# Moving the attention logits one row further ahead on TensorE, and signalling the normed rows by halves

## The chip, the core and the metric

The kernel runs on one core of a Trainium2 chip. The metric is device time in microseconds (us) for one execution. Five engines work side by side, each through its own list of instructions in order: TensorE (PE in the profile: matrix products and transposes; PEld is its loading of weights), VectorE (DVE), ScalarE (ACT), GpSimd (POOL) and SyncE (SP, which issues DMA transfers). They meet only at semaphores: one instruction counts a semaphore up when it is done, another waits for a count.

## What is computed

One layer of a streaming encoder over 1024 rows of 1024 features, all in float32. Cut to the part around the change:

```python
h = rms_norm(x, mix_norm_g)
u_a, v_a, q, k, v = split(h @ w_in)
y_a = spatial_gating(u_a, v_a, ...)
# sliding-window attention, 8 heads, chunks of 64 rows, windows of 128 keys
logits = einsum(q, k) * 64 ** -0.5 + bias
p = softmax with a learned sink per head (logits)
y_b = einsum(p, v)
x = x + concat(rms_norm(y_a), rms_norm(y_b)) @ w_out
h = rms_norm(x, ffn_norm_g)
x = x + (silu(h @ w_gate) * (h @ w_up)) @ w_down
return rms_norm(x, final_norm_g)
```

## The kernel before, in words

The program is written by hand, engine by engine: each engine's function is a straight list of calls, and their order in the source is the order on the engine. The 1024 rows are 8 row tiles of 128 (T = 8). A product of two float32 matrices is made of three matmuls of rounded parts (`split_mm`, lines 853 to 855).

After the input projection comes a loop over the row tiles r = 0 to 7, the output stage, in which the attention of coming rows, the output projection of rows r and r+1 and the transposes of the normed row r-1 are interleaved. On TensorE one turn of it, for r from 1 to 5, is:

- `probs_T(r+1, 0)`, `out_unit(r+1, 0)`, `probs_T(r+1, 1)`: the probabilities of row r+1 transposed in two parts (line 1033), with 12 matmuls of the output projection between them (`out_unit`: the first half of the features, `ya`, against `woA`, units 0 and 1; the second, `yb`, against `woB`, units 2 and 3).
- `yb_rows(r)`: one transpose (line 1051) for the norm of the attention's output.
- `logits(r+2)`: 8 small products of queries and keys (line 1021), into two PSUM banks.
- `h2_transposed(r-1, 0)`: four transposes of the first 512 columns of the normed row `x2n` (line 1116).
- `out_unit(r+1, 1)`, `values(r+1)` (probabilities times values, line 1044), `h2_transposed(r-1, 1)` (the other 512 columns), `out_unit(r, 2)`, `out_unit(r, 3)`.

The turn r = 0 has only `out_unit(1, 1)`, `values(1)`, `out_unit(0, 2)`, `out_unit(0, 3)`; its logits stand ahead of the loop. The turn r = 6 has no logits.

On VectorE the same turn is `norm_x2(r-1)` (line 2036: row r-1 times its root and gain, 1024 columns into `x2n`), `add_out(r+1, 0)` (line 2024: a projected half added into the row `xr`), `yb_totals(r)` (line 2006), `add_bias(r+2)` (line 1973: the logits read out of PSUM into the tile `S`) and `maxima(r+2)` (lines 1984 to 1988), `h2_lo(r-1, 0)` (line 2043, or 2049 from row 4 on: what is left of the transposed row after rounding), `add_out(r+1, 1)`, `yb_lo(r+1)` (line 2002), `add_out(r, 2)`, `normal_probs(r+2)` (lines 1993 to 1998, which end with `S` ready to be transposed), `h2_lo(r-1, 1)`, `add_out(r, 3)`. In the turn r = 0, `woB_piece` (line 2010) and `ya_lo_rows` (line 1883) stand among them.

A row's way from projection to transposes is a chain over four engines: `out_unit(r, 3)` on PE, `add_out(r, 3)` on DVE, `x2_square(r)` on ACT (line 1502), the root on POOL (lines 647 and 649), `norm_x2(r)` on DVE, `h2_transposed(r, 0)` on PE.

The waits that count here:

- `h2_transposed(r, kh)` waits for `x2n_ready` at r+1 (the last row, r = 7, has a signal `x2n_half` of its own for kh = 0), and for the PSUM bank: `h2_ready` at 2r + kh, which `h2_lo` of the part before counts up, since all these transposes go through bank 7.
- `logits(r)` waits for `s_added` at 2r + 1, that is, until `add_bias(r-1)` has read the two banks.
- `probs_T(r, 0)` waits for `pn_ready` at r+1, from `normal_probs(r)`.

Of the kernel before, what the change touches and what calls it, by code (L numbers as in the profile page):

```python
# [24 lines left out]
def hybrid_trunk_layer(nc, x, xT, mix_gT, w_in, sgu_ln_g, sgu_ln_b, sgu_w, sgu_b, sinks, rel_bias,  # L25
                       group_norm_g, w_out, ffn_norm_g, w_gate, w_up, w_down, final_norm_g, out):
    F32, F32R = mybir.dt.float32, mybir.dt.float32r
    ALU, ACT, AX = mybir.AluOpType, mybir.ActivationFunctionType, mybir.AxisListType
    P = 128
    ROWS, D = x.shape  # L30
    T = ROWS // P
# [16 lines left out]
    C = 512  # L48
# [5 lines left out]
    def at(name, kb, shape, dtype=F32):  # L54
        n = 4
        for s in shape[1:]:
            n *= s
        offset = BASE + int(kb * 1024)
        assert offset + n <= nc.sbuf_usable_end, name
        return nc.alloc_sbuf_tensor_at(name, shape, dtype, offset=offset)  # L60
# [60 lines left out]
    xr = [at(f"xr{s}", a, [P, D]) for s, a in enumerate((160, 164, 26))]  # L121
    x2n = at("x2n", 196.25, [P, D])
    ffn_gB = at("ffn_gB", 202, [P, D])
# [64 lines left out]
    ssq2, ms2, rstd2 = late[:, 0:T], late[:, T:2 * T], late[:, 2 * T:3 * T]  # L188
# [51 lines left out]
    def added_at(p, i):  # L240
        return 4 * ADDED.index(p) + i + 1

    def corner_at(p, i):
        return 4 + 4 * CORNERS.index(p) + CORNER_ORDER[p].index(i) + 1
# [17 lines left out]
    def out_at(r, n):  # L262
        return OUT.index((r, n)) + 1
# [37 lines left out]
    with ExitStack() as ctx:  # L301
        ps = ctx.enter_context(nc.psum_tensor("ps", [P, 8, C], F32))

        def sem(name):
            return ctx.enter_context(nc.semaphore(name))
# [36 lines left out]
        out_done, out_added, x2_sq, ms2_ready, rstd2_ready, x2n_ready, h2_T, h2_ready = (  # L342
            sem(n) for n in ("out_done", "out_added", "x2_sq", "ms2_ready", "rstd2_ready", "x2n_ready", "h2_T",
                             "h2_ready"))
# [12 lines left out]
        x2n_half = sem("x2n_half")  # L357
# [491 lines left out]
        def _(pe):  # L849
# [157 lines left out]
            def logits(r):  # L1007
                if r == 0:
                    pe.wait_ge(c_out, corner_at("P3", 1))
                    pe.wait_ge(vwin_ready, 4)  # L1010
                else:
                    pe.wait_ge(s_added, 2 * r + 1)
                if r == HT:
                    pe.wait_ge(c_out, corner_at("P4", 1))
                for ci in range(2):
                    c = 2 * r + ci
                    for tp in range(2):
                        for g in range(KV):
                            rows = slice(g * DH, (g + 1) * DH)
                            q = qT[r // HT][rows, c % (NCH // 2), 2 * tp:2 * tp + 2, :].rearrange("p t q -> p (t q)")  # L1020
                            last = mm(ps[:, 3 + g, (2 * ci + tp) * P:(2 * ci + tp + 1) * P], q, kT[rows, c * CH:c * CH + WIN],  # L1021
                                      start=True, stop=True)
                last.then_inc(logits_done, 1)

            def probs_T(r, ci):
                pe.wait_ge(pn_ready, r + 1)
                if r == 0 and ci == 0:
                    pe.wait_ge(c_summed, added_at("P3", 2))
                if ci == 1:
                    pe.wait_ge(pT_ready, 2 * r + 1)  # L1030
                for g in range(KV):
                    for tp in range(2):
                        last = nc.tensor.transpose(ps[:, 5, (2 * g + tp) * P:(2 * g + tp + 1) * P], S[:, g, ci, tp, :], ident[:])  # L1033
                last.then_inc(p_T, 1)

            def values(r):
                pe.wait_ge(pT_ready, 2 * r + 2)
                if r:
                    pe.wait_ge(yb_totalled, r)
                else:  # L1040
                    pe.wait_ge(c_summed, added_at("P3", 3))
                for ci in range(2):
                    for g in range(KV):
                        last = mm(ps[g * DH:(g + 1) * DH, 6, ci * G * CH:(ci + 1) * G * CH], V2[:, 2 * r + ci, g, :], pT[:, ci, g * G * CH:(g + 1) * G * CH],  # L1044
                                  start=True, stop=True)
                last.then_inc(pv_done, 1)
# [29 lines left out]
            def out_unit(r, n):  # L1076
                u = out_at(r, n) - 1
                h = n % 2
                if u >= 3:
                    pe.wait_ge(out_added, u - 2)  # L1080
                else:
                    pe.wait_ge(c_out, corner_at("P4", u))
                if n < 2:
                    if u == 0:
                        pe.wait_ge(wo_split, HA)
                    if r % HT == 0:
                        pe.wait_ge(ya_ready, 8 if r else 4)
                    lhs = [ya[:, r, hl] for hl in range(2)]
                    rhs = (woA_hi, woA_lo)
                else:  # L1090
                    pe.wait_ge(yb_ready, r + 1)
                    lhs = [yb[r % 2][:, hl] for hl in range(2)]
                    rhs = (woB_hi, woB_lo)
                cs = slice(h * C, (h + 1) * C)
                for k in range(4):
                    if n == 2 and r == 0:
                        pe.wait_ge(wo_split, HA + k + 1)
                    last = split_mm(ps[:, u % 3, :], (lhs[0][:, k, :], lhs[1][:, k, :]), (rhs[0][:, k, cs], rhs[1][:, k, cs]), k == 0, k == 3)
                last.then_inc(out_done, 1)

            def h2_transposed(r, kh):
                if r == T - 1 and kh == 0:
                    pe.wait_ge(x2n_half, 1)
                else:
                    pe.wait_ge(x2n_ready, r + 1)
                if r == T - 2 and kh:
                    pe.wait_ge(out_added, out_at(T - 2, 3))
                elif r == T - 1:
                    pe.wait_ge(out_added, out_at(T - 1, 2 + kh))
                elif r or kh:  # L1110
                    pe.wait_ge(h2_ready, 2 * r + kh)
                else:
                    pe.wait_ge(ssqA_ready, 2)
                for k in range(4):
                    a = (4 * kh + k) * P
                    last = nc.tensor.transpose(ps[:, H2_BANK[r, kh], k * P:(k + 1) * P], x2n[:, a:a + P], ident[:])  # L1116
                last.then_inc(h2_T, 1)
# [9 lines left out]
            for r in range(T):  # L1127
                if 0 < r < T - 1:
                    probs_T(r + 1, 0)
                    out_unit(r + 1, 0)  # L1130
                    probs_T(r + 1, 1)
                    yb_rows(r)
                if 0 < r < T - 2:
                    logits(r + 2)
                if r + 1 < T:
                    if 0 < r < T - 2:
                        h2_transposed(r - 1, 0)
                    out_unit(r + 1, 1)
                    if r == T - 2:
                        h2_transposed(r - 1, 0)  # L1140
                    values(r + 1)
                    if 0 < r < T - 2:
                        h2_transposed(r - 1, 1)
                out_unit(r, 2)
                if r == T - 2:
                    h2_transposed(r - 1, 1)
                if r == T - 2:
                    yb_rows(r + 1)
                out_unit(r, 3)
# [597 lines left out]
        def _(dve):  # L1747
            tt, ts, stt = nc.vector.tensor_tensor, nc.vector.tensor_scalar, nc.vector.scalar_tensor_tensor
# [277 lines left out]
            def norm_x2(r):  # L2026
                if r == 0:
                    dve.wait_ge(ffng_in, 16)
                else:
                    dve.wait_ge(h2_T, 2 * r)  # L2030
                dve.wait_ge(rstd2_ready, r + 1)
                if r == T - 1:
                    stt(x2n[:, 0:C], xr[r % 3][:, 0:C], rstd2[:, r:r + 1], ffn_gB[:, 0:C], ALU.mult, ALU.mult).then_inc(x2n_half, 1)
                    stt(x2n[:, C:D], xr[r % 3][:, C:D], rstd2[:, r:r + 1], ffn_gB[:, C:D], ALU.mult, ALU.mult).then_inc(x2n_ready, 1)
                    return
                stt(x2n[:], xr[r % 3][:], rstd2[:, r:r + 1], ffn_gB[:], ALU.mult, ALU.mult).then_inc(x2n_ready, 1)

            def h2_lo(r, kh):
                flat = "p k n -> p (k n)"
# [74 lines left out]
            for r in range(T):  # L2114
                if r:
                    norm_x2(r - 1)
# [32 lines left out]
            weight_lo(0, "P2", 0)  # L2149
            weight_lo(0, "P6", 0)  # L2150
            norm_x2(T - 1)
            h2_lo(T - 2, 0)
            h2_lo(T - 2, 1)
# [158 lines left out]
```

## Time and profile before

| | before |
|---|---|
| median of 3 runs | 927.34 us (927.29 to 927.34) |
| the profiled execution: time | 927.43 us |
| the profiled execution: span on the core | 925.6 us |
| PE busy | 913.2 us, 99% of the span |
| PEld, DVE, ACT, POOL busy | 81%, 64%, 47%, 43% |
| granted TensorE clock | 0.998 of full speed |
| output stage, the turns r = 1 to 5 | 190.1 to 267.0 us of the span |

The profile lists for every engine the instructions with start and length, what ended an idle time before them, and the granted clock. The trace has two records for a float32 matmul that is no product of rounded parts, so 8 products of the source are 16 there. Its matmuls overlap: a start is when one enters the array, and the next may enter before it has left, so what counts for PE is the distance from start to start.

### The profile page before, as it was taken

Reading aid. Unit: us, or ns where it says so; the run is one execution under the profiler, and the core shown is the slowest. Engines: PE = TensorE matmul, PEld = TensorE weight load, DVE = VectorE, ACT = ScalarE, POOL = GpSimd, SP = SyncE. Lnnn points to the kernel's source line nnn. Section 1 sums busy time; section 2 is a strip of 40 time slices with the busy share of each in tenths; the row PEclk is TensorE's granted clock in tenths of the full one; section 3 lists DMA queues with packets and bytes.
Section 4 is the critical chain, followed back from the end, with each engine's and each line's share of the span. In section 5 each row is a group of like instructions: output and inputs, shape, how many; then the busy total and the mean of one; then the engine's idle time right before and its main releaser. Section 6 shows DMA issues by size and latency. Waiting matters only on the chain.

```text
span 925.6 us, 11960 instructions
## 1 busy us (share of the span) xinstructions
PE 913.2 (99%) x4229; PEld 748.9 (81%) x4229; DVE 588.2 (64%) x776; ACT 430.5 (47%) x837; POOL 402.2 (43%) x392
## 2 busy tenths in 40 slices
PE   9999999899999999999999999999999999999997
PEld 7888887677878878888888888888888888888885
DVE  5659878877677876364464745646446666544753
ACT  6647547775655633332333333333334354444351
POOL 2459633622224388566585564955754000000022
PEclk9999999999999999999999999999999999999999
DMA  9787454112233352725527355273457996656543
GB/s 332 252 242 229 115 162 145 35 57 80 89 108 101 114 170 92 243 88 194 174 98 240 99 174 183 91 239 121 152 190 265 350 385 197 199 189 199 187 139 133
DMA packets 151487, 158.56 MB, mean 171 GB/s; under 512 B 27576, under 2 KB 109060, under 8 KB 151428
## 3 DMA queue, kind: packets, MB, share of 16 engines
q1 hardware_dynamic: 150756, 157.40, 52.5%
q8 instruction: 34, 0.56, 0.2%
q10 hardware_dynamic: 672, 0.40, 0.1%
q14 instruction: 25, 0.20, 0.1%
HBM read 117.26 MB, written 40.50 MB: 170 GB/s over the span
## 4 chain that ended last, share of the span: by engine, by line
PE 87%; DVE 4%; issue 3%; ACT 3%; POOL 2%; DMA 1%; DVEq 0%; POOLq 0%; ACTq 0%
PE ps L853 27%; PE ps L855 27%; PE ps L854 27%; ACT S L1451 1%; PE ps L969 1%; PE ps L1044 1%; PE ps L1116 1%; PE ps L1021 1%; PE ps L1033 1%; DVE P_lo L2086 1%; DMA A22s<-in_w_gate 1%; DVE woA_lo L1780 0%; POOL V L714 0%; PE ps L877 0%; DVE T_lo L2073 0%
## 5 line engine op out<-in xcount | busy, mean ns | idle before, releaser
L2086 DVE TENSOR_TENSOR P_lo<-P_raw,P_hi 128x512 fp32r<-128x512 f32 x132 | 120.8, 931 | 83.5 <-ACT P_hi L1545 76.2
L853 PE MATMUL ps<-T_hi,P_hi 128*128 128x512 f32 x352 | 137.1, 390 | 0.0
L855 PE MATMUL ps<-T_hi,P_lo 128*128 128x512 f32 x352 | 137.0, 389 | 0.0
L854 PE MATMUL ps<-T_lo,P_hi 128*128 128x512 f32 x352 | 136.9, 389 | 0.0
L797 POOL TENSOR_TENSOR wd<-wd 128x256 f32<-128x256 f32 x88 | 81.2, 923 | 93.8 <-DMA wd<-in_w_down 88.6
L853 PE MATMUL ps<-rb_hi,ra_hi 128*128 128x512 f32 x308 | 119.8, 389 | 0.0
L854 PE MATMUL ps<-rb_lo,ra_hi 128*128 128x512 f32 x308 | 119.8, 389 | 0.0
L855 PE MATMUL ps<-rb_hi,ra_lo 128*128 128x512 f32 x308 | 119.8, 389 | 0.0
L1659 ACT ACTIVATE ra_hi<-ra 128x512 fp32r<-128x512 f32 x77 | 48.6, 632 | 98.4 <-DMA rb<-w_down_T 59.6
L647 POOL TENSOR_SCALAR late<-late 128x1 f32<-128x1 f32 x12 | 5.5, 458 | 193.4 <-ACT junk L1727 177.2
L2182 DVE TENSOR_TENSOR ra_lo<-ra,ra_hi 128x512 fp32r<-128x512 f32 x77 | 55.2, 718 | 37.2 <-ACT ra_hi L1659 37.0
L1545 ACT ACTIVATE P_hi<-P_raw 128x512 fp32r<-128x512 f32 x132 | 76.6, 620 | 3.5 <-POOL P_raw L756 3.5
L853 PEld LDWEIGHTS ps<-T_hi,P_hi 128*128 128x128 f32 x352 | 66.1, 188 | 14.3 <-issue 0.7
L855 PEld LDWEIGHTS ps<-T_hi,P_lo 128*128 128x128 f32 x352 | 66.1, 188 | 13.9
L854 PEld LDWEIGHTS ps<-T_lo,P_hi 128*128 128x128 f32 x352 | 66.1, 188 | 13.6
L1650 ACT ACTIVATE G<-G 128x512 f32<-128x512 f32 x33 | 20.9, 632 | 112.4 <-DVE G L2162 112.4
L853 PE MATMUL ps<-B,P_hi 128*128 128x512 f32 x176 | 69.0, 392 | 0.1
L855 PE MATMUL ps<-B,P_lo 128*128 128x512 f32 x176 | 68.5, 389 | 0.0
L854 PE MATMUL ps<-B,P_hi 128*128 128x512 f32 x176 | 68.5, 389 | 0.0
L854 PEld LDWEIGHTS ps<-rb_lo,ra_hi 128*128 128x128 f32 x308 | 57.8, 188 | 12.1
L853 PEld LDWEIGHTS ps<-rb_hi,ra_hi 128*128 128x128 f32 x308 | 57.8, 188 | 12.1
L855 PEld LDWEIGHTS ps<-rb_hi,ra_lo 128*128 128x128 f32 x308 | 57.8, 188 | 11.8
(272 smaller groups left out, 2028.0 us busy)
## 6 DMA issues: line engine op xcount, KB each, us to landing
wd<-in_w_down SPq DMA_DIRECT2D x44, 256.0 KB, 3.4
w_down_T<-wd SPq DMA_DIRECT2D x22, 512.0 KB, 4.8
ra<-act_S SPq DMA_DIRECT2D x44, 256.0 KB, 2.7
rb<-w_down_T SPq DMA_DIRECT2D x44, 256.0 KB, 3.0
act_S<-Q SPq DMA_DIRECT2D x33, 256.0 KB, 3.7
ra<-act_A SPq DMA_DIRECT2D x33, 256.0 KB, 4.9
rb<-in_w_down SPq DMA_DIRECT2D x33, 256.0 KB, 5.7
P_raw<-in_w_gate SPq DMA_DIRECT2D x22, 256.0 KB, 3.6
```

What stands on the lines that cost most here:

```text
L797: nc.gpsimd.tensor_tensor(wd[:, d, :], wd[:, x, :], wd[:, y, :], ALU.subtract).then_inc(wd_summed, 1)
L853: mm(dst, lhs[0], rhs[0], start=start, stop=False, skip_group_check=onto)
L854: mm(dst, lhs[0], rhs[1], start=False, stop=False, skip_group_check=onto)
L855: return mm(dst, lhs[1], rhs[0], start=False, stop=stop, skip_group_check=onto)
L969: last = mm(ps[:, MIX_BANK[m % 2], t * P:(t + 1) * P], vn[:, h, HT * half + t], sgu_wT[:, h, :], start=True, stop=True)
L1021: last = mm(ps[:, 3 + g, (2 * ci + tp) * P:(2 * ci + tp + 1) * P], q, kT[rows, c * CH:c * CH + WIN], start=True, stop=True)
L1033: last = nc.tensor.transpose(ps[:, 5, (2 * g + tp) * P:(2 * g + tp + 1) * P], S[:, g, ci, tp, :], ident[:])
L1545: actv(w_h[p, m][:], src[:], ACT.Copy).then_inc(w_hi_ready, 1)
L1650: actv(g[:], g[:], ACT.Silu).then_inc(silu_done, 1)
L1659: actv(ra_hi[n][:], ra[n][:], ACT.Copy).then_inc(step_hi, 1)
L2086: tt(w_l[p, m][:], src[:], w_h[p, m][:].bitcast(F32), ALU.subtract).then_inc(w_split, 1)
L2182: tt(ra_lo[n][:], ra[n][:], ra_hi[n][:].bitcast(F32), ALU.subtract)
```

## The change

Two things are edited. On TensorE the call of `logits` moves: in the turn r it was `logits(r+2)` behind `yb_rows(r)`; now it is `logits(r+3)` behind `values(r+1)`, also in the turn r = 0, and not in the turn r = 5. On VectorE `norm_x2` writes its row in two halves of 512 columns for every row, the first of which counts up `x2n_half`, the second `x2n_ready`; `h2_transposed(r, 0)` waits for the first. The places of the transposes in the list stay as they are.

```diff
             def h2_transposed(r, kh):
-                if r == T - 1 and kh == 0:
-                    pe.wait_ge(x2n_half, 1)
+                if kh == 0:
+                    pe.wait_ge(x2n_half, r + 1)
                 else:
                     pe.wait_ge(x2n_ready, r + 1)
...
                     yb_rows(r)
-                if 0 < r < T - 2:
-                    logits(r + 2)
                 if r + 1 < T:
...
                     values(r + 1)
+                    if r + 3 < T:
+                        logits(r + 3)
                     if 0 < r < T - 2:
                         h2_transposed(r - 1, 1)
...
                 dve.wait_ge(rstd2_ready, r + 1)
-                if r == T - 1:
-                    stt(x2n[:, 0:C], xr[r % 3][:, 0:C], rstd2[:, r:r + 1], ffn_gB[:, 0:C], ALU.mult, ALU.mult).then_inc(x2n_half, 1)
-                    stt(x2n[:, C:D], xr[r % 3][:, C:D], rstd2[:, r:r + 1], ffn_gB[:, C:D], ALU.mult, ALU.mult).then_inc(x2n_ready, 1)
-                    return
-                stt(x2n[:], xr[r % 3][:], rstd2[:, r:r + 1], ffn_gB[:], ALU.mult, ALU.mult).then_inc(x2n_ready, 1)
+                stt(x2n[:, 0:C], xr[r % 3][:, 0:C], rstd2[:, r:r + 1], ffn_gB[:, 0:C], ALU.mult, ALU.mult).then_inc(x2n_half, 1)
+                stt(x2n[:, C:D], xr[r % 3][:, C:D], rstd2[:, r:r + 1], ffn_gB[:, C:D], ALU.mult, ALU.mult).then_inc(x2n_ready, 1)
```

On PE in the turn r = 0 the list around `values(1)` gains the logits of row 3 (a line number, the result and the operands stand in each row; `qT_152` holds the queries of rows 0 to 3, `qT_153` those of rows 4 to 7):

```order
 L855 MATMUL ps<-woA_hi,ya 128x512
 L1044 MATMUL ps<-pT,V_154 64x256 x4
+L1021 MATMUL ps<-kT,qT_152 128x128 x8
 L853 MATMUL ps<-woB_hi,yb_158 128x512
 L854 MATMUL ps<-woB_lo,yb_158 128x512
```

The eight products stand now between the values and the first matmul of `out_unit(0, 2)`.

On PE in the turn r = 1, and in the same way in r = 2 to 4, the row of logits goes from between `yb_rows` and the first transposes of `x2n`:

```order
 L1033 MATMUL ps<-ident,S 128x128 x4
 L1051 MATMUL ps<-ident,yb_sum_162 128x128
-L1021 MATMUL ps<-kT,qT_152 128x128 x8
 L1116 MATMUL ps<-ident,x2n 128x128 x4
 L853 MATMUL ps<-woA_hi,ya 128x512
```

The transposes of `x2n` follow directly on the single transpose of `yb_rows`. In the turn r = 5 the same row goes too, and none comes back behind its values.

On DVE, the row `x2n` of r = 0 (in the turn r = 1; the others alike):

```order
 L1883 TENSOR_TENSOR ya<-vn,ya 128x4x128 x4
-L2036 SCALAR_TENSOR_TENSOR x2n<-xr_172,late,ffn_gB 128x1024
+L2032 SCALAR_TENSOR_TENSOR x2n<-xr_172,late,ffn_gB 128x512
+L2033 SCALAR_TENSOR_TENSOR x2n<-xr_172,late,ffn_gB 128x512
 L2024 SCALAR_TENSOR_TENSOR xr_174<-ps,small,xr_174 128x512
 L2006 TENSOR_REDUCE small<-ps 128x1
```

One instruction of 1024 columns is now two of 512; ACT, POOL and SP keep their lists.

## Rows read from the trace of the kernel before

**Rows 1.** The page: busy time of each engine.

```profile
PE 913.2 (99%) x4229; PEld 748.9 (81%) x4229; DVE 588.2 (64%) x776; ACT 430.5 (47%) x837; POOL 402.2 (43%) x392
```

**Rows 2.** Waits between 170 and 290 us: us in total, times, longest.

```profile
PE ps L1051 <- POOL yb_sum L774: 2.0, 1, 2.0
...
PEld ps L1033 <- DVE S L1998: 0.9, 2, 0.5
...
PEld ps L853 <- DVE woB_lo L2010: 0.4, 1, 0.4
PE ps L1116 <- DVE x2n L2036: 0.2, 1, 0.2
```

**Rows 3.** The stretch of turn 3: length, busy PE, PEld, DVE, ACT, POOL, clock.

```profile
220.99:236.26 15.27, 15.27 (x91) 12.10 (x89) 10.37 (x18) 9.21 (x28) 3.48 (x7) 1.00 0.19 70
```

**Rows 4.** Timeline of PE, turn 3: start, us, line, operation.

```profile
224.63 0.27 PE L1051 MATMUL ps<-ident,yb_sum 128*128 128x128 f32 x1
224.83 1.16 PE L1021 MATMUL ps<-kT,qT 64*128 64x128 f32 x16
225.92 0.66 PE L1116 MATMUL ps<-ident,x2n 128*128 128x128 f32 x4
...
229.27 1.08 PE L1044 MATMUL ps<-pT,V 128*64 128x256 f32 x8
230.29 0.66 PE L1116 MATMUL ps<-ident,x2n 128*128 128x128 f32 x4
```

**Rows 5.** Timeline of DVE, turn 3.

```profile
224.27 1.29 DVE L2036 SCALAR_TENSOR_TENSOR x2n<-xr,late,ffn_gB 128x1024 f32<-128x1024 f32 x1 [2.22 <-POOL late L649]
225.47 0.75 DVE L2024 SCALAR_TENSOR_TENSOR xr<-ps,small,xr 128x512 f32<-128x512 f32 x1
...
226.33 1.28 DVE L1973 TENSOR_TENSOR S<-ps,bias 128x512 f32<-128x512 f32 x2
...
229.18 0.68 DVE L2043 TENSOR_TENSOR B<-ps,B 128x512 fp32r<-128x512 f32 x1
```

**Rows 6.** Timeline of POOL, turn 3, behind the root of line 649.

```profile
226.50 0.19 POOL L647 TENSOR_SCALAR small<-small 128x1 f32<-128x1 f32 x1 [2.34 <-DVE small L2006]
```

**Rows 7.** Timeline of PE, turns 0 and 1.

```profile
185.83 0.40 PE L854 MATMUL ps<-woB_lo,yb 128*128 128x512 f32 x1
186.07 0.39 PE L855 MATMUL ps<-woB_hi,yb 128*128 128x512 f32 x1
186.44 0.50 PE L853 MATMUL ps<-woB_hi,yb 128*128 128x512 f32 x1
...
189.75 0.39 PE L855 MATMUL ps<-woB_hi,yb 128*128 128x512 f32 x1
190.10 0.66 PE L1033 MATMUL ps<-ident,S 128*128 128x128 f32 x4
...
193.99 1.16 PE L1021 MATMUL ps<-kT,qT 64*128 64x128 f32 x16
195.39 0.65 PE L1116 MATMUL ps<-ident,x2n 128*128 128x128 f32 x4 [0.24 <-DVE x2n L2036]
```

**Rows 8.** Timeline of DVE: turn 0, turn 1 and the last row.

```profile
181.06 1.28 DVE L1973 TENSOR_TENSOR S<-ps,bias 128x512 f32<-128x512 f32 x2
...
194.04 1.28 DVE L2036 SCALAR_TENSOR_TENSOR x2n<-xr,late,ffn_gB 128x1024 f32<-128x1024 f32 x1 [0.52 <-POOL late L649]
...
291.55 1.78 DVE L2033 SCALAR_TENSOR_TENSOR x2n<-xr,late,ffn_gB 128x512 f32<-128x512 f32 x1
293.26 0.74 DVE L2034 SCALAR_TENSOR_TENSOR x2n<-xr,late,ffn_gB 128x512 f32<-128x512 f32 x1
293.92 0.68 DVE L2049 TENSOR_TENSOR T_raw<-ps,T_raw 128x512 f32<-128x512 f32 x1
```

**Rows 9.** Timeline of turn 5: the second transposes on PE, and DVE.

```profile
260.82 0.66 PE L1116 MATMUL ps<-ident,x2n 128*128 128x128 f32 x4
...
259.72 0.68 DVE L2049 TENSOR_TENSOR T_raw<-ps,T_raw 128x512 f32<-128x512 f32 x1
```

## The prediction

> **What bounds the kernel now.** I began with the page: PE is busy 913.2 us of a span of 925.6 [rows 1]. A change can only gain where PE stands still, and can only lose by making it stand. So I then asked for PE's waits in the output stage, where the edits lie [rows 2]. Between 170 and 290 us there are three of note: 2.0 us for `yb_sum` ahead of the loop, which the change doesn't touch, a few tenths for `S` and `woB_lo`, and 0.2 us for `x2n`, once. The windows by turn say the same: turn 3 lasts 15.27 us and PE is busy in all of it [rows 3]. What the change may win is thus well under 1 us; the question is what it may lose. For that I laid the timelines of PE and DVE beside each other.
>
> In turn 3 the single transpose of `yb_rows` starts at 224.63, the logits at 224.83, the first transposes of `x2n` at 225.92 [rows 4]. `x2n` itself is written from 224.27 for 1.29 us, to 225.56 [rows 5]; the writing waited 2.22 us for POOL's root, which hangs on the row's last projection on PE. So the row is ready only 0.36 us before PE asks for it, and it is the 1.09 us of logits (225.92 less 224.83) that cover it.
>
> **Taking the cover away.** The change moves these 1.09 us behind `values`, past the first transposes. No matmul is added or dropped, and a product costs the same at either place unless the neighbours matter (a rival below). But the chain from the last projection of row r-1 to `x2n` is as long as it was, while PE now reaches the transposes 1.09 us earlier against it: at 224.83 in the times of this trace.
>
> **What the halves give back.** The first half is one instruction of 512 columns. Its like in the last row took 0.74 us [rows 8], and `add_out`, of the same kind and size, 0.75 [rows 5]. The other end is the last row's first half, 1.78 us, which ran beside work of POOL [rows 8]; in turn 3 POOL has nothing to do for 2.34 us behind the root [rows 6], so I take 0.75. From the end of such a write to the start of PE there were 0.07 us in turn 1 (194.04 and 1.28 make 195.32, PE at 195.39 [rows 7, 8]). So the transposes start at 224.27 + 0.75 + 0.07 = 225.09, and PE waits 225.09 - 224.83 = 0.26 us where it waited for nothing. Turns 2 to 5 have the same pattern: 4 times 0.26 is 1.04 us. Bounds: 0 if PE is held up by something else until then, 4 times 1.3 if every first half took 1.78.
>
> Turn 1 has less time in hand, since the root came late: PE would arrive at 193.99, and the half is there at 194.04 + 0.75 + 0.07 = 194.86, a wait of 0.87. What goes is the old wait, 195.39 less 195.08 (193.99 and 1.09), 0.31. Net 0.56 us.
>
> **The second half and what is behind it on DVE.** The pair costs more than one write. In the last row the second half started 0.07 before the first had ended, and the next instruction 0.66 after the second's start [rows 8]; a pair of 0.75 thus holds DVE for 0.68 + 0.66 = 1.34, where the whole row held it from 224.27 to 225.47, 1.20 [rows 5]. That is 0.14 us a row for all that is queued behind: `add_out`, `add_bias`, `maxima`, `h2_lo`. The Trainium skill (VectorE: DVE Perf Modes, The DRAIN you can't avoid) says that the next operation doesn't start until the pipe of the one before is empty. By that the pair would hold DVE 0.07 us longer than I reckon, and the one term below in which the pair counts would be 0.69 instead of 0.62; the overlap in the last row speaks against it. Nobody but `h2_lo` is met by PE soon after. It ends at 229.86 in turn 3 [rows 5], 230.07 with the pair and the signal; PE comes to the second transposes at 230.29 less 0.83 (the transposes start that much earlier) plus 1.09 for the logits now in front of them, 230.55. Hidden, by 0.5.
>
> Turn 5 is different: the logits of row 7 were done in turn 4, so none stand in front of the second transposes. PE comes at 260.82 - 0.83 = 259.99; the `h2_lo` it must await ends at 259.72 + 0.68 = 260.40 [rows 9], with 0.14 and 0.07 at 260.61. A wait of 0.62 us. The ends: 0, if DVE gets there sooner, and 0.9, if the transposes lose their 0.26 too.
>
> **What the move wins.** In turn 0, `out_unit(0, 2)` now comes 1.09 us later, when the last piece of `woB_lo` is done. The wait for it was 0.14 us by PE's own starts (0.37 between 186.07 and 186.44, against 0.24 before it [rows 7]) and 0.4 on the weight loads [rows 2]; I take 0.2. Before the next `probs_T` there are 0.35 us from 189.75 to 190.10 [rows 7], 0.12 more than the usual distance, a wait for `S`. It goes as well, since DVE catches up. Together 0.32.
>
> **Waits that the moved logits add.** They need `add_bias(r+2)` done: in turn 3 at 226.33 + 1.28 = 227.61, and PE comes behind `values` at 229.5; in turn 0 at 182.34 [rows 8], and PE at 184.1. Nothing. DMA issues and ACT's and POOL's lists stay; SP's waits for logits are met earlier and stand behind waits for whole rows.
>
> **The sum:** 1.04 + 0.56 + 0.62 - 0.32 = +1.90 us. Nothing later takes it up: behind the loop PE works without waits, and all that it needs hangs on the same rows. The profiled execution took 927.43 us, span 925.6 and 1.8 around it; that makes 929.33. The median of the runs lies 0.09 lower, so I forecast **929.2 us**, 0.2% slower. About 0.2% (1.85 us) is also what a measurement of this kernel can tell from no change: my forecast stands on that edge.
>
> **Rivals.**
> *The halves close the gap.* If PE reaches the first transposes a quarter of a microsecond later than I reckon, or the half is quicker, turns 2 to 5 wait for nothing; then turn 5's second wait is 0.62 + 0.26, and the sum 0.56 + 0.88 - 0.32 = 1.12, 928.4 us: not slower by what can be told. For it speaks that 0.26 is small; against, that the half's 0.75 is measured and that the transpose of `yb_rows` takes only 0.20 [rows 4]. The Trainium skill (Perfetto Trace Analysis, Optimizing Scalar/DVE Operations) backs it: if Vector causes bubbles on other engines, breaking up its instructions may allow work to be completed sooner. By that rule the splitting decides; the rows say that it shortens PE's way by 0.53 us while the move takes 1.09 of cover.
> *The softmax starts sooner*, as logits a row ahead would suggest, and PE's waits for `S` (0.9 us on the weight loads, two of them [rows 2]) vanish with nothing lost: 926.8. Against it: `add_bias` doesn't wait for logits now; DVE runs from `x2n` to it without idle time [rows 5].
> *Neighbours cost.* `values` and logits use the array in other shapes than the transposes. From `values` to the transposes there are 1.02 us, and from the single transpose of `yb_rows` to the logits 0.20 [rows 4]. If the step from `values` to logits pays such a 0.20 once more, the four turns with moved logits lose 0.8, 930.0; at twice that 930.8. It decides wherever the start-to-start is above 1.02.
> *POOL slows the first half* as in the last row: five turns of 1.03, 934. POOL's idle time speaks against it.
>
> **How the numbers follow.** My forecast has 0.62, with its own range 928.6 to 929.8, a little under half of it beyond the edge of 929.2. The closed gap has 0.15, the early softmax 0.03, the neighbours 0.15, POOL or another delay 0.05. Slower: 0.28 + 0.15 + 0.05 = 0.48. Faster by over 0.2% would need 925.5, more than all waits of rows 2 that the change can reach: 0.02. The same: the rest, 0.50. The range 928.0 to 930.6 takes in the closed gap and most of the neighbours.
>
> **What would show it.** In the changed profile: waits of PE's line 1116 for the first half of `x2n` in turns 1 to 5, about 0.9 and four times 0.26; one of some 0.6 for `h2_lo` in turn 5; turns 2 to 4 at 15.5 us instead of 15.27; no wait for `woB_lo`. It is wrong if turns stay at 15.27, if the logits behind `values` take clearly more than 1.09, or if DVE's `add_bias` starts earlier after the row's last projection.

## The result and the profile after

| | before | with the change |
|---|---|---|
| median | 927.65 us (926.87 to 928.58, 21 runs) | 928.95 us (928.14 to 930.49, 21 runs) |
| ratio of the times | | 1.0016, 95% interval 1.0009 to 1.0022 |
| profiled execution: span | 925.6 us | 927.1 us |
| PE busy | 913.2 us, 99% | 912.8 us, 98% |
| granted TensorE clock | 0.998 | 0.996 |

The kernel became slower by 0.8 to 2.0 us. The sum gave 1.90; the forecast of 929.2 lies 0.25 above the median, on a median of before that was 0.3 higher than the three runs shown earlier. Against the 0.2% that the prediction named as the bound of what can be told, the median ratio is just inside "the same"; with 21 runs of each kernel the interval is finer than that bound, and shows a small loss.

The page after has the same instructions on PE, and seven more on DVE for the seven rows now written in two parts:

```profile
span 927.1 us, 11967 instructions
...
PE 912.8 (98%) x4229; PEld 749.5 (81%) x4229; DVE 584.1 (63%) x783; ACT 430.5 (46%) x837; POOL 398.3 (43%) x392
```

The view of waits, PE's rows between 160 and 292 us (us in total, times, longest one), answers to [rows 2]:

```profile
PE ps L1051 <- POOL yb_sum L774: 2.0, 1, 2.0
PE ps L1116 <- DVE x2n L2032: 1.5, 5, 0.8
PE ps L1033 <- ACT pT L1463: 1.1, 1, 1.1
...
PE ps L1116 <- DVE T_raw L2046: 0.7, 1, 0.7
```

Line 1116, the transposes of `x2n`, waited once before, for 0.2 us. Now it waits for the first half (line 2032) five times and once for `h2_lo` (line 2046).

The timelines of turn 3, PE first and then DVE, answer to [rows 4, 5] (start, us, instruction, idle time before it):

```profile
226.36 0.27 PE L1051 MATMUL ps<-ident,yb_sum 128*128 128x128 f32 x1
226.82 0.66 PE L1116 MATMUL ps<-ident,x2n 128*128 128x128 f32 x4 [0.18 <-DVE x2n L2032]
230.15 1.08 PE L1044 MATMUL ps<-pT,V 128*64 128x256 f32 x8
231.16 1.16 PE L1021 MATMUL ps<-kT,qT 64*128 64x128 f32 x16
232.26 0.66 PE L1116 MATMUL ps<-ident,x2n 128*128 128x128 f32 x4
```

```profile
226.01 0.75 DVE L2032 SCALAR_TENSOR_TENSOR x2n<-xr,late,ffn_gB 128x512 f32<-128x512 f32 x1 [2.22 <-POOL late L649]
226.68 0.75 DVE L2033 SCALAR_TENSOR_TENSOR x2n<-xr,late,ffn_gB 128x512 f32<-128x512 f32 x1
227.34 0.74 DVE L2024 SCALAR_TENSOR_TENSOR xr<-ps,small,xr 128x512 f32<-128x512 f32 x1
```

The first half takes 0.75 us and PE starts at 226.82, 0.06 behind its end; the pair holds DVE for 1.33 (226.01 to 227.34), where 1.34 was reckoned. DVE waits 2.22 us for POOL's root as before. The step from `values` to the logits is 1.01 us, from the logits to the transposes 1.10: the neighbours cost nothing. Turns 2 to 4 last 15.54, 15.51 and 15.52 us by the starts of their first transposes; before it was 15.27.

One thing in this profile is not of the change. Behind the 2.0 us wait for `yb_sum`, ahead of turn 0, the matmuls come 0.42 us apart for a while. The windows of that stretch, after the change and then before it (length, busy PE, PEld, DVE, ACT, POOL, granted clock, DMA):

```profile
178.90:182.30 3.40, 3.40 (x12) 2.62 (x10) 3.22 (x5) 0.00 (x0) 1.97 (x4) 0.53 0.02 5
```

```profile
180.20:183.00 2.80, 2.80 (x14) 2.12 (x12) 2.62 (x5) 0.00 (x0) 1.52 (x4) 1.00 0.02 6
```

The same code runs at a granted clock of 0.53, nearly all of it at the lower level of 1.2 GHz, in one profile and at 1.00 in the other. From `yb_rows(0)` to `values(1)` it is 5.04 us after and 3.43 before, 1.61 more. The spans of these two profiles can therefore not be compared as they stand. Their difference of 1.5 us is made of four parts: the profile after reaches the end of the wait 1.28 us earlier (178.37 against 179.65), in code that the edits do not touch; it loses the 1.61; it loses 1.47 from `values(1)` to line 1055 at the end of the output stage; and it is 0.3 shorter behind that. Two experiments below hold the clock still.

### The profile page after: what moved, and what is told of

Read it like the earlier page. It is cut to its first block, busy times and chain, and to the rows that moved or that the text cites. A ratio compares the mean times of both kernels' runs of the same rounds, so it can differ in the third digit from the quotient of the medians.

```text
span 927.1 us, 11967 instructions
## 1 busy us (share of the span) xinstructions
PE 912.8 (98%) x4229; PEld 749.5 (81%) x4229; DVE 584.1 (63%) x783; ACT 430.5 (46%) x837; POOL 398.3 (43%) x392
## 4 chain that ended last, share of the span: by engine, by line
PE 86%; DVE 4%; issue 4%; ACT 3%; POOL 2%; DMA 1%; DVEq 0%; POOLq 0%; ACTq 0%
PE ps L853 27%; PE ps L855 27%; PE ps L854 27%; PE ps L1021 1%; PE ps L969 1%; PE ps L1044 1%; ACT x2n L1502 1%; PE ps L1116 1%; ACT S L1451 1%; DVE P_lo L2083 1%; DVE x2n L2032 1%; DMA A22s<-in_w_gate 1%; DVE woA_lo L1780 0%; PE ps L1033 0%; POOL late L649 0%
## 5 line engine op out<-in xcount | busy, mean ns | idle before, releaser
L2083 DVE TENSOR_TENSOR P_lo<-P_raw,P_hi 128x512 fp32r<-128x512 f32 x132 | 117.1, 903 | 84.8 <-ACT P_hi L1545 77.9
```

What stands on the lines that cost most here:

```text
L2083: tt(w_l[p, m][:], src[:], w_h[p, m][:].bitcast(F32), ALU.subtract).then_inc(w_split, 1)
```

## The experiments

Besides the time, one distance is used: from the start of `values(1)` in turn 0 to the transposes of `yb_raw` (line 1055) in turn 6, all on PE. It was 95.38 us before and 96.85 after.

**The halves alone.** The logits stay where they were; `norm_x2` and the wait are those of the change.

```diff
-                if r == T - 1 and kh == 0:
-                    pe.wait_ge(x2n_half, 1)
+                if kh == 0:
+                    pe.wait_ge(x2n_half, r + 1)
...
-                stt(x2n[:], xr[r % 3][:], rstd2[:, r:r + 1], ffn_gB[:], ALU.mult, ALU.mult).then_inc(x2n_ready, 1)
+                stt(x2n[:, 0:C], xr[r % 3][:, 0:C], rstd2[:, r:r + 1], ffn_gB[:, 0:C], ALU.mult, ALU.mult).then_inc(x2n_half, 1)
+                stt(x2n[:, C:D], xr[r % 3][:, C:D], rstd2[:, r:r + 1], ffn_gB[:, C:D], ALU.mult, ALU.mult).then_inc(x2n_ready, 1)
```

> Only the halves, the logits stay behind yb_rows. Measure beside the time: the stage from the start of values(1) to the transposes of yb_raw (line 1055), 95.38 us before (183.08 to 278.46) and 96.85 with the whole change (183.41 to 280.26). Theory (the move takes away the cover of the chain to x2n, the halves give part of it back): with the cover in place the halves have next to nothing to win. The wait of turn 1 (0.31) goes, but the second transposes of that turn then wait for h2_lo, which the pair puts 0.14 later; stage 95.4, within 0.2 of before, time within 0.03% of before. Rival (the pair's 0.14 on DVE is what costs, in every turn): stage 96.0 or more. Rival (the halves win by themselves): stage 95.1 or less.

Measured: 927.31 us, ratio to before 0.9998 (0.9989 to 1.0007); distance 95.51. No wait for `x2n` is left, and the view of waits has in its place

```profile
PE ps L1033 <- DVE S L1998: 0.5, 2, 0.3
PE ps L1116 <- DVE B L2040: 0.3, 1, 0.3
```

The first row is in turns 0 and 6; the second is the wait of turn 1's second transposes, as expected: by the starts, the halves win 0.32 us ahead of the first transposes of turn 1, and the later `h2_lo` costs 0.31 ahead of the second. With the cover in place the halves win nothing in all.

**The move alone.** The logits as in the change, `x2n` written whole for rows 0 to 6.

```diff
-                if 0 < r < T - 2:
-                    logits(r + 2)
...
                     values(r + 1)
+                    if r + 3 < T:
+                        logits(r + 3)
```

> Only the move of the logits, x2n written whole for rows 0 to 6. Theory: PE now waits for the whole row: turns 2 to 5 lose 0.80 each (x2n ends 1.29 after its start instead of 0.75), turn 1 1.09, no wait for h2_lo in turn 5, and 0.6 won in turns 0 and 6; together +3.7, stage 99.1, time 0.4% above before. Rival (the move costs by its neighbours on the array, whatever x2n does): stage as with the whole change, 96.9. Rival (the move is harmless, the pair costs): stage 95 or less.

Measured: 933.9 us, ratio 1.007 (1.0057 to 1.0083); distance 101.13. The move by itself costs 6.3 us by the medians, and 5.75 by the distance, which leaves out the slow stretch that this profile has too; 3.7 were expected. The waits:

```profile
PE ps L1116 <- DVE x2n L2036: 4.4, 5, 1.3
...
PE ps L1033 <- DVE S L1998: 1.2, 4, 0.3
```

The first row is the expected one: 0.77 to 0.79 us in turns 2 to 5, 1.30 in turn 1. The second was not expected, and the timelines of turn 2 show where it comes from, DVE first and then POOL:

```profile
222.56 0.75 DVE L2024 SCALAR_TENSOR_TENSOR xr<-ps,small,xr 128x512 f32<-128x512 f32 x1 [1.91 <-PE ps L855]
223.22 0.66 DVE L1993 TENSOR_TENSOR small<-small 128x8 f32<-128x8 f32 x1
...
224.15 1.32 DVE L1998 TENSOR_TENSOR S<-S,small 128x1024 f32<-128x1024 f32 x1
```

```profile
223.12 0.74 POOL L770 TENSOR_TENSOR yb_sq<-yb_sq 128x256 f32<-128x256 f32 x1 [7.78 <-ACT yb_sq L1482]
```

An operation on 8 columns, which took 0.16 to 0.17 us in all eight rows before, takes 0.66, until POOL's sum (223.12 to 223.86) is over. That pushes `S` back by 0.5, and `probs_T` waits for `S`: by the starts on PE it costs 0.5 us in each of four turns, which is the 2 us by which the expectation fell short. Before, DVE was already in the multiplication of `S` when POOL's sum came, and POOL was the one held up (1.54 us in turn 2).

**Turn 5's second transposes later.** The change, with

```diff
-                    if 0 < r < T - 2:
+                    if 0 < r < T - 3:
                         h2_transposed(r - 1, 1)
                 out_unit(r, 2)
-                if r == T - 2:
+                if T - 3 <= r < T - 1:
                     h2_transposed(r - 1, 1)
```

> The whole change, with one call more moved: in turn 5 the second transposes of x2n come behind out_unit(5, 2) instead of ahead of it. Theory: the 0.65 us wait for h2_lo in turn 5 goes and nothing takes its place: stage 96.2 (96.85 less 0.65), about 0.8 above before. Rival (the wait only moves on, to what hangs on the later transposes): stage stays near 96.8.

Measured: 928.25 us, ratio 1.0011 (1.0002 to 1.002); distance 96.73. The wait for `h2_lo` is gone and turn 5 takes 14.53 us instead of 15.10. The distance fell by only 0.12, because turn 0 is 0.52 longer in this profile (8.20 us from `values(1)` to `probs_T(2, 0)`, 7.68 with the change): this profile has no slow stretch, and PE waits 0.33 us for `S` there. Against the filled kernel with the change below, whose turn 0 is as long (8.19), the distance is 0.55 shorter (97.28 and 96.73): the wait went and did not move on.

**The first transposes later, in all turns.** As the last, and

```diff
-                    if 0 < r < T - 2:
-                        h2_transposed(r - 1, 0)
                     out_unit(r + 1, 1)
-                    if r == T - 2:
+                    if r:
                         h2_transposed(r - 1, 0)
```

> As e3, and in turns 1 to 5 the first transposes come behind out_unit(r+1, 1), 2.9 us of matmuls later. Theory: all waits for x2n go (turn 1's 0.76, the 0.18 to 0.25 of turns 2 to 5), what the move wins in turns 0 and 6 stays: stage 94.4, time about 0.9 us below before and 2.4 below the change. Rival (the wait goes over to the second transposes, since ACT's copies and h2_lo start later; 0.1 to 0.3 a turn): stage 95 to 95.6.

Measured: 926.39 us, ratio 0.9986 (0.9978 to 0.9995); distance 95.09. No wait for `x2n` is left: with 2.9 us of matmuls in front of the transposes the chain is covered again, and the 1.5 us of these waits in the profile after are gone. The distance is 0.7 above the expected one, by waits for `S` in turns 0 and 6 and one of 0.41 for `h2_lo` in turn 1. It is the first version faster than both kernels; the slow stretch is not in this profile. Part of the gain by the medians is the clock: 10 of these 11 runs have a mean granted clock of 0.998 or more, and only 11 of the 27 of the kernel before. Among such runs alone the medians are 926.37 and 927.00, a gain of 0.6.

**The 2.0 us wait filled, before and after.** In the kernel before, and in the changed one, the wait for `yb_sum` gets matmuls:

```diff
             probs_T(1, 1)
+            pe.wait_ge(ssqA_ready, 1)
+            for n in range(8):
+                mm(ps[:, 7, :], ya[:, 0, 0, n % 4, :], woA_hi[:, n % 4, 0:C], start=True, stop=True)
             yb_rows(0)
```

> The kernel before, with 8 matmuls of 512 columns added on PE ahead of yb_rows(0), whose results nobody reads; they stand in the 2.0 us in which PE waits there for POOL's yb_sum, and take 1.8. It tests a theory on the clock: in three of six profiles so far (the change, e1, e2) the matmuls after this wait come 0.43 us apart instead of 0.23 for some 3.5 us, which costs 1.6; in three (before, e3, e4) they don't. Theory: it is the wait that brings the clock down, by chance of when it falls; with the wait filled no profile has the slow stretch, the median falls by about half of 1.6 (0.5 to 0.8 us below before), and the times of the executions scatter less. Rival (the slow stretch has another cause): the same median as before or later by up to 0.3, the same scatter, a slow stretch in some profiles.

> The whole change with the same 8 matmuls. Theory: again no slow stretch, so that the difference between this and the filled kernel before is the change alone: 1.9 us by the prediction's sum, 1.3 to 2.0 by the marks of the profiles so far; start of turn 1 to line 1055 in the profile 89.2 against 88.4. Rival (the change's loss was mostly the slow stretch): the two filled kernels differ by less than 0.7.

Measured: 926.4 us for the kernel before (11 runs, 926.06 to 927.46; ratio to before 0.9991, 0.9982 to 1.0) and 928.1 for the changed one (11 runs, 927.6 to 928.57; ratio to before 1.0007, 0.9998 to 1.0016). Neither profile has the slow stretch. The windows of it, before and then changed:

```profile
176.60:182.30 5.70, 5.53 (x29) 4.31 (x28) 3.96 (x6) 1.12 (x2) 3.76 (x6) 1.00 0.02 3
```

```profile
176.60:182.30 5.70, 5.53 (x28) 4.10 (x26) 3.96 (x6) 0.93 (x2) 3.73 (x7) 1.00 0.01 3
```

The times scatter over 1.4 and 1.0 us in 11 runs each. Without filling it is 1.5 in the 21 runs of the kernel before that belong to these, and 2.4 in the 21 of the changed one, so that the scatter alone says little for the kernel before. Eight matmuls more made the kernel before 0.9 us faster by the medians (926.4 against 927.29 in the same runs), though the interval just touches no change. Among runs with a mean granted clock of 0.998 or more alone it is 0.5 (all 11 with the filling, 12 of the 21 without), so the clock is part of it; the rest was not followed. Between the filled kernels the medians differ by 1.7 us and the distances by 97.28 - 95.38 = 1.90. With the clock the same, that is the change alone. Behind line 1055 the changed kernel is 0.4 us shorter (646.8 us to the end of the span, 647.2 in the kernel before).

**Turn 0 in another order.** On top of the version with the late transposes: `out_unit(1, 1)` ahead of `yb_rows(0)` on PE, `add_bias(2)` and `maxima(2)` ahead of `yb_totals(0)` on DVE, and the second transposes late in turn 1 too.

```diff
             probs_T(1, 1)
+            out_unit(1, 1)
             yb_rows(0)
...
-                    out_unit(r + 1, 1)
                     if r:
+                        out_unit(r + 1, 1)
                         h2_transposed(r - 1, 0)
...
-                    if 0 < r < T - 3:
+                    if 1 < r < T - 3:
                         h2_transposed(r - 1, 1)
                 out_unit(r, 2)
-                if T - 3 <= r < T - 1:
+                if r in (1, T - 3, T - 2):
                     h2_transposed(r - 1, 1)
...
+                if r == 0:
+                    add_bias(2)
+                    maxima(2)
                 if r + 1 < T:
                     yb_totals(r)
...
-                if r + 2 < T:
+                if 0 < r < T - 2:
                     add_bias(r + 2)
                     maxima(r + 2)
```

> e4, with the 2.0 us wait used: on PE out_unit(1, 1) comes ahead of yb_rows(0) and the transposes of ya_totals; on DVE add_bias(2) and maxima(2) come ahead of yb_totals(0) in turn 0; in turn 1 too the second transposes come behind out_unit(1, 2). Theory: PE's wait for yb_sum goes and the softmax of row 2 no longer hangs behind it: 1.5 to 2.0 us in turn 0, 0.4 in turn 1, and no slow stretch: 2 to 3 us below e4, about 924 us. Rival (DVE's backlog in turn 0 is the bound: the wait moves to values(1) or to probs_T(2, 0)): within 0.6 of e4.

Measured: 923.74 us, ratio 0.9962 (0.9949 to 0.9974), 2.65 below the version with the late transposes, as expected. The wait for `yb_sum` is gone, one of 0.7 for `yb_totals` stands in `values(1)`:

```profile
PE ps L1044 <- DVE small L2005: 0.7, 1, 0.7
```

**The first logits earlier too.**

```diff
-            probs_T(0, 1)
             logits(1)
+            probs_T(0, 1)
```

> e7, and ahead of the loop logits(1) come in front of probs_T(0, 1), where PE waits 1.1 us for ACT's copy of the first probabilities. Theory: the 1.09 us of logits fill that wait: 1.0 below e7. Rival (what hangs on probs_T(0, 1), the copy and values(0), comes as late as it did and PE waits there instead): the same as e7.

Measured: 923.01 us, ratio 0.9953 (0.994 to 0.9965), 0.7 below the last by the medians, with intervals that overlap. PE's 1.1 us wait in `probs_T(0, 1)` became one of 0.7 in `values(0)`:

```profile
PE ps L1044 <- ACT pT L1462: 0.7, 1, 0.7
```

So part of it moved on, as the rival had it. This is the fastest version.

## Why the prediction was right

The mechanism, a cover taken away and half given back, held in turns 1 to 5. Two other steps failed, what turn 0 wins and that nothing later takes the loss up, and the total came out in part by luck: the stage's 1.90 us is what the filled kernels show to the last digit, but with terms that were off and cancel. By the starts on PE in the two filled profiles, from `values(1)` on:

| up to | before | change | added since the row above | predicted |
|---|---|---|---|---|
| `probs_T(2, 0)`, end of turn 0 | 7.00 | 8.19 | 1.19 | 1.09 - 0.32 = 0.77 |
| first transposes of turn 1 | 12.29 | 12.80 | -0.68 | 0.87 - 0.31 - 1.09 = -0.53 |
| first transposes of turn 5 | 73.36 | 74.87 | 1.00 | 4 x 0.26 = 1.04 |
| second transposes of turn 5 | 77.73 | 79.94 | 0.70 | 0.62 |
| `probs_T(7, 0)` | 83.94 | 85.88 | -0.27 | 0 |
| line 1055 | 95.38 | 97.28 | -0.04 | 0 |

- **The cover.** Right: the move alone makes PE wait 0.77 us and more for the whole row, the halves bring that to 0.18 as the view of waits counts it, and 0.25 a turn of start-to-start.
- **What the halves give back.** Right: 0.75 us for the half and 0.06 for the signal, 0.75 and 0.07 predicted. The halves alone changed nothing (0.9998): they are worth something only where the cover is gone.
- **The pair on DVE and turn 5.** Right in place, 0.08 too small: the wait for `h2_lo`, 0.63 in the filled changed kernel, costs 0.70 start to start.
- **What the move wins in turn 0.** This step failed. Its term was -0.32, and the filled kernels show +0.10 (1.19 less 1.09). The wait for `woB_lo` did go, but "DVE catches up" did not hold: in the filled changed kernel PE waits 0.34 us for `S` ahead of `probs_T(2, 0)`.

```profile
PE ps L1033 <- DVE S L2001: 0.3, 1, 0.3
```

  In the filled kernel before, DVE's short operation and then POOL's sum stood like this:

```profile
187.80 0.17 DVE L1996 TENSOR_TENSOR small<-small 128x8 f32<-128x8 f32 x1
```

```profile
188.29 1.77 POOL L770 TENSOR_TENSOR yb_sq<-yb_sq 128x256 f32<-128x256 f32 x1 [5.42 <-ACT yb_sq L1485]
```

  DVE and then POOL in the filled changed kernel:

```profile
187.50 0.75 DVE L2027 SCALAR_TENSOR_TENSOR xr<-ps,small,xr 128x512 f32<-128x512 f32 x1 [0.62 <-PE ps L855]
188.16 0.70 DVE L1996 TENSOR_TENSOR small<-small 128x8 f32<-128x8 f32 x1
...
189.13 1.32 DVE L2001 TENSOR_TENSOR S<-S,small 128x1024 f32<-128x1024 f32 x1
```

```profile
188.10 0.74 POOL L770 TENSOR_TENSOR yb_sq<-yb_sq 128x256 f32<-128x256 f32 x1 [5.43 <-ACT yb_sq L1485]
```

  The logits put `add_out(0, 2)` and what follows it later, so that POOL's sum came first and the 8-column operation took 0.70 us. The profiles of turn 5 later and of the transposes later, with moved logits and the clock at 1.00 too, show the same turn 0 (8.20 and 8.19 us). Where the slow stretch came first, in the profile after and in the move alone, POOL's sum was over when DVE came (188.78 and 189.23 us in the profile after), and the move did win 0.43 and 0.42 there. Of what the clash cost, 0.15 came back in turn 1, where the wait for the half was 0.72 start to start instead of 0.87.
- **Turn 6.** Not in the sum: before, `probs_T(7, 0)` waited for `S`, whose multiplication took 1.61 us there; with the change it took 1.23 and the wait went, 0.27 us. Its row in the kernel before:

```profile
265.36 1.61 DVE L1998 TENSOR_TENSOR S<-S,small 128x1024 f32<-128x1024 f32 x1
```

- **Nothing later takes it up.** This step failed too. From line 1055 to the end of the span it is 646.8 us in all seven profiles with the halves and 647.1 to 647.2 in the three without them, 0.3 to 0.4 won. Some 0.24 of it is at the transposes of the last row, from whose start to the next matmul it is 1.03 us before and 0.79 after; the chain that brings this about was not followed.
- **The rivals.** The closed gap is out: the waits are there. The earlier softmax is out: DVE still starts `add_bias` from `x2n` on, without idle time, and nothing was won (the 0.9 us of waits that this rival names would give 926.4, not the 926.8 it states). The neighbours cost nothing. POOL did not slow the first halves.

The medians' +1.3 us lies 0.6 below the sum of 1.90, the filled kernels' +1.7 lies 0.2 below. The 0.3 to 0.4 won behind line 1055 leave 1.5 to 1.6 of the sum, and the runs with the clock at its upper level agree: among runs with a mean granted clock of 0.998 or more the medians are 928.48 us with the change (9 of 21) and 927.0 and 926.9 before (11 of 27 and 12 of 21, taken beside the experiments), 1.5 to 1.6 apart. The interval of the measurement (0.8 to 2.0 us) holds the sum as well, but does not tell these apart.

## What to carry to other kernels

A piece of work on the engine that bounds a kernel can have a second use: it covers a chain that runs on other engines. Before moving it, compare when the chain's result is there with when the engine would now ask for it; here, in turns 2 to 5, 1.09 us of cover went, 0.29 of it had been to spare, splitting gave 0.54 back, and 0.25 a turn stayed lost. When the transposes were put behind 2.9 us of matmuls instead, both moves together became a small gain, 0.3 us by the distance.

## What the runs showed of the hardware

Three of the six profiles without filling or reordering (the change, the halves alone, the move alone) have PE at the lower clock level for part of the stretch behind the 2.0 us wait, three (before, turn 5 later, transposes later) have not, with the same instructions ahead of it. From `yb_rows(0)` to `values(1)` it is 5.03 to 5.04 us in the first three and 3.43 to 3.44 in the others, 1.6 us.

The mean granted clocks that are on record with the runs show that the scatter of the times goes with it. These six profiles have a mean granted clock of 0.996 to 0.997 with the slow stretch and 0.998 without. Of the 21 runs of the changed kernel, the 12 at 0.996 took 928.93 to 930.49 us and the 9 at 0.998 or more 928.14 to 928.85. Of the 21 runs of the kernel before beside the filled kernels, 9 at 0.996 or 0.997 took 927.67 to 928.17 and 12 at 0.998 or more 926.64 to 927.30. Where the wait is filled or gone (both filled kernels and the two versions with turn 0 reordered), all 32 runs have 0.998 or more. The loss by the medians, about 1.0 us, is less than the 1.6 of the stretch. What decides it from one execution to the next was not found.

A DVE operation on two tiles in SBUF and POOL's sum of two such tiles shut each other out, and who comes first decides: 0.16 us became 0.66 to 0.70 for DVE's short operation, and POOL's 0.74 became 1.25 to 1.77 behind DVE's multiplication in the kernel before. The Trainium skill (SBUF — State Buffer, SBUF: two separate sides) says that a DVE instruction with two inputs in SBUF and a GpSimd instruction that reads SBUF share a pair of ports under an exclusive lock, and that the later one blocks until the earlier is done. The trace agrees: in the move alone the short operation ended at 223.88, and POOL's at 223.86. A shift of half a microsecond on PE can thus change who waits.
